# The gates' transposes ahead of the value projection, in an encoder step on one core

## The reference

```python
qm, km, vm, om, gates, cq, ckv, kr = jnp.split(h @ w_in, idx, axis=-1)
ig = gates[..., :M_HEADS]
lf = jax.nn.log_sigmoid(gates[..., M_HEADS:])
# mLSTM, per block of frames: decays from the running sum of lf, stabilised by a running max
b = jnp.cumsum(lf, axis=-1)
m = jnp.maximum(b + m0[..., None], jnp.max(D, axis=-1))
num = w_inter[..., None] * (q @ C0) + S @ v
h = num / jnp.maximum(jnp.abs(den), jnp.exp(-m))[..., None]
```

## Time and profile before

| | us |
|---|---|
| median of 3 runs | 3267.42 |
| lowest, highest | 3266.88, 3267.92 |
| the profiled execution | 3267.42 |
| its span, first to last instruction | 3265.6 |
| TensorE busy in the span | 3005.4 |
| VectorE busy | 1281.1 |
| GpSimd busy | 1000.2 |
| ScalarE busy | 561.5 |

### The profile page before, as it was taken

The page is one execution under the profiler, slowest core; times in us unless marked ns, Lnnn a source line. Parts: engine busy times, 40 slices in busy tenths (PEclk is TensorE's granted clock), DMA queues, the critical chain, the costliest instruction groups (busy, mean ns, idle before and its releaser), DMA issues.

```text
span 3265.6 us, 42745 instructions
## 1 busy us (share of the span) xinstructions
PE 3005.4 (92%) x17374; PEld 2777.7 (85%) x17374; DVE 1281.1 (39%) x1366; ACT 561.5 (17%) x844; POOL 1000.2 (31%) x474
## 2 busy tenths in 40 slices
PE   4999998988899999999879998999979999999995
PEld 3988876678799999999869987666869999999995
DVE  3433344543633323233473334355354323233326
ACT  2211233431200000000132213144221000000001
POOL 1222242224133343333312223233223433333430
PEclk9999988999999999999989999799989999999997
DMA  5112210011011111111122212000211111111111
GB/s 144 35 35 32 37 41 1 1 73 45 26 45 45 39 51 45 45 45 45 30 80 42 34 28 34 28 1 7 86 33 33 51 45 45 45 45 39 51 39 53
DMA packets 210335, 137.11 MB, mean 42 GB/s; under 512 B 49256, under 2 KB 201384, under 8 KB 209712
## 3 DMA queue, kind: packets, MB, share of 16 engines
q1 hardware_dynamic: 184672, 103.97, 12.4%
q10 hardware_dynamic: 25552, 31.64, 2.8%
HBM read 119.64 MB, written 15.94 MB: 42 GB/s over the span
## 4 chain that ended last, share of the span: by engine, by line
PE 87%; DVE 3%; DVEq 3%; ACT 3%; issue 2%; ACTq 1%; POOL 0%; POOLq 0%; DMA 0%
PE acc L493 18%; PE acc L497 17%; PE acc L496 17%; PE acc L897 5%; PE acc L901 5%; PE acc L900 5%; PE acc L842 3%; DVEq L1277 2%; PE acc L472 2%; PE acc L473 2%; PE acc L474 2%; PE acc L714 1%; PE acc L621 1%; PE acc L605 1%; PE acc L524 1%
## 5 line engine op out<-in xcount | busy, mean ns | idle before, releaser
L493 PE MATMUL acc<-act_hi,slab_hi 128*128 128x352 f32 x2928 | 964.0, 329 | 63.6 <-DVE act_lo L1262 25.8
L497 PE MATMUL acc<-act_lo,slab_hi 128*128 128x352 f32 x2928 | 950.1, 324 | 0.0
L496 PE MATMUL acc<-act_hi,slab_lo 128*128 128x352 f32 x2928 | 947.7, 324 | 0.0
L371 POOL TENSOR_TENSOR slab_hi<-slab_raw,ones 128x1024 fp32r<-128x1024 f32 x148 | 281.7, 1904 | 1285.6 <-PE acc L493 691.2
L493 PEld LDWEIGHTS acc<-act_hi,slab_hi 128*128 128x128 f32 x2928 | 556.1, 190 | 80.6 <-issue 60.2
L497 PEld LDWEIGHTS acc<-act_lo,slab_hi 128*128 128x128 f32 x2928 | 558.5, 191 | 0.0
L496 PEld LDWEIGHTS acc<-act_hi,slab_lo 128*128 128x128 f32 x2928 | 557.4, 190 | 0.0
L1619 DVE TENSOR_TENSOR branch<-acc,branch 128x1056 f32<-128x1056 f32 x176 | 221.4, 1258 | 410.3 <-PE acc L901 410.3
L373 POOL TENSOR_TENSOR slab_lo<-slab_raw,slab_hi 128x1024 fp32r<-128x1024 f32 x148 | 367.9, 2486 | 21.1
L1609 DVE TENSOR_TENSOR work<-acc,work 128x1056 f32<-128x1056 f32 x44 | 55.3, 1257 | 599.4 <-PE acc L497 599.4
L371 POOL TENSOR_TENSOR small_hi<-slab_raw,ones 128x1024 fp32r<-128x1024 f32 x46 | 88.8, 1931 | 510.4 <-PEq L904 369.5
(11 more groups left out here) (328 smaller groups left out, 4302.0 us busy)
## 6 DMA issues: line engine op xcount, KB each, us to landing
slab_raw<-in_w_ffn_in SPq DMA_DIRECT2D x88, 512.0 KB, 3.6
slab_raw<-in_w_ffn_out SPq DMA_DIRECT2D x44, 512.0 KB, 3.4
slab_raw<-in_w_in SPq DMA_DIRECT2D x40, 512.0 KB, 4.9
x_spill<-residual ACTq DMA_DIRECT2D x2, 4224.0 KB, 13.0
residual<-x_spill ACTq DMA_DIRECT2D x2, 4224.0 KB, 12.6
slab_raw<-in_w_out SPq DMA_DIRECT2D x16, 512.0 KB, 3.9
branch<-in_x_prompt ACTq DMA_DIRECT2D x4, 1024.0 KB, 9.3
out_y_prompt<-branch ACTq DMA_DIRECT2D x8, 512.0 KB, 3.0
```

What stands on the lines that cost most here:

```text
L371: pool.tensor_tensor(hi, raw, ONES[:, 0:1].broadcast_to([P, SLAB]), ALU.mult)
L493: mm = pe.matmul(out, wh, HH[:, x], start=k == 0, stop=False)
L496: pe.matmul(out, wl, HH[:, x], start=False, stop=False)
L497: mm = pe.matmul(out, wh, HL[:, x], start=False, stop=k == KT - 1)
```

## The change

In TensorE's program the value product, `first_pair(2, 0, 1, 2, (2,))`, is called after the gates' transposes and selections instead of before them. This holds for both layers, since the call stands in the layers' loop. The wait for gate_exps and the wait for set 1 go with the transposes.

```diff
                 first_pair(0, 2, 0, 1, ())
 
-                first_pair(2, 0, 1, 2, (2,))
                 pe.wait_ge(gate_exps, l * 4 + 4)
                 wait_set(l, 1, 1)
                 for c in range(CH):
                     mm = pe.transpose(PS[:, 3 * BANK + c * P:3 * BANK + (c + 1) * P], X[:, G4 + c * P:G4 + (c + 1) * P], IDN[:, :])
                 for j in range(PAIRS):
                     mm = pe.matmul(bank(6, CH, off=j * CH), SEL[:, j * P:(j + 1) * P], SMALL[0:8, 40:40 + CH], start=True, stop=True)
                 mm.then_inc(gate_turned, 1)
+                first_pair(2, 0, 1, 2, (2,))
                 first_pair(3, 1, 1, 3, (0,))
                 pe.drain().then_inc(slab_free[1], 1)
```

## The result

The changed kernel is slower: a median of 3302.8 us over four timed runs (3300.0 to 3306.0) against 3267.2 us (3266.9 to 3267.9) on the same chip, ratio 1.0108, 95% interval 1.0096 to 1.0120. That is 35.6 us more, where 29.1 were forecast; it lies above the range of 3291 to 3301. Its profiled execution took 3305.8 us, with a span of 3304.0.

The account below looks back on a forecast made before the run. TensorE, busy 92% of the span, was taken to bound the kernel. Stand, transposes, value product, lost cover and clock made 14.6 us in layer 0 and 14.5 in layer 1: 3267.4 + 14.6 + 14.5 = 3296.5, range 3291 to 3301.

Parts of the forecast that it names:

- The direction: Whole kernel: slower, given a chance of 0.96, against 0.03 for the same and 0.01 for faster.
- the clock: TensorE after the stand, each layer: half clock for 4.6 us (3.0 to 6.0), 2.1 us lost.
- the later stretches: Rest of the kernel: gains or losses from clock falls landing elsewhere, 1 us to either side.
- The stand: TensorE before the gates' transposes, layer 0: idle from 111.28 to 123.60, 12.3 us, waiting for the gates.
- The gates' time of 123.54: End of ScalarE's last gate row, L1032, in layer 0: expected to stay at 123.54 despite the change.
- The value product: TensorE, behind transposes and selections: 11.39 us from first to last matmul start at full clock.
- the lost cover: Before the output-gate product: transposes no longer hide ScalarE's emptying of set 0; 1.47 us from last to first start.
- the path: TensorE from the query product to the output-gate product: the forecast's steps without the clock term, 12.5 us a layer.
- The rival of a longer half clock: Restart after the stand: half clock not left while transposes run, 1.6 us a layer more, 3299.7 in all; chance 0.07.
- The earlier gates: Rival: VectorE and ScalarE run faster while TensorE stands, gates come up to 2 us earlier, 3292; chance 0.06.
- the overtaking: Rival: TensorE passes the waiting transposes and runs the value product, time 3267.4; not slower had chance 0.03.

Follow-up runs that it names:

- warm: Changed kernel with 70 unused matmuls of 128x352 between the query product and the gates' wait; 3289.7 us, ratio 1.0063 to the kernel before.
- turns4: Changed kernel with the gates' nine transposes done four times over, only the last nine counting; a single run, 3292.6 us.
- select_later: Changed kernel with only the four selections moved behind the value product, the transposes staying ahead; 3297.1 us, ratio 1.0083 to the kernel before.
- plain: Changed kernel with the gates' nine transposes done as ordinary float32 matmuls against the identity; 3299.3 us, ratio 1.0096 to the kernel before.

## Why the prediction was wrong

The direction, the wait and the order of size were right. One term of the sum, the clock, was mis-sized, and what the later stretches add was put too low.

- The stand: 12.3 us forecast, 12.31 and 12.29 measured. The gates' time of 123.54 held, counted from the query product: L1032 ended 12.15 us after L1026 began, before 12.21.
- The value product and the lost cover: right. The wait for L1015 is 1.14 us, as taken from the earlier trace rows, and layer 0 of `warm` shows the path without the clock at 12.5 us, as in the sum.
- **The clock: this is the step that failed.** The forecast took 4.6 us at half clock, 2.1 us lost, from four restarts that all began with dense products. Measured are 9.6 and 9.1 us. The excess over the path is 3.91 - 2.06 on the gates' block and 14.07 - 11.39 on the product, 4.5 us in layer 0 and 4.4 in layer 1, where 2.1 were forecast. The price of a microsecond at half clock held (0.46 forecast, 4.5 / 9.6 = 0.47 measured); its length did not. That is 4.7 us too little in two layers (33.8 against 29.1).
- The rival of a longer half clock had the right sign and two thirds of the size (8.0 us in place of 4.6, 1.6 us a layer, where 2.4 and 2.3 were missing), but only 0.07, and its reason was wrong as stated. I had taken from the earlier trace rows that transposes bring the clock up, and two layers of `turns4` confirmed it, after 6.1 and 5.7 us. The Trainium skill ("TensorE: Matmul & The Clock Gate", Part 4) says that work in transpose mode does not count as activity that brings the clock up; `turns4` shows the contrary. With that I stopped, and did not ask what the rest of the restart looked like. Behind nine transposes come eight passes of 9 columns. `select_later` moved only these and had the clock back after 6.1 us; `plain` changed the mode and had it down for 9.4. The half clock of 20.5 us at 450.6, over narrow passes and without a stand, was in the trace that I had.
- The later stretches: forecast at 1 us to either side. The profiled pair shows 4.6 us more in them, 3.8 of it in one late split; the timed runs of the result show 35.6 - 33.8 = 1.8 us. I had not looked at what a shift of TensorE does to the meeting of GpSimd's split with VectorE's small steps, although the row at 249.49 was in the trace of before. That this comes with the change is not shown: the kernel before has such a case too, and they move from run to run.
- The earlier gates and the overtaking: both fell. ScalarE's last row kept its length (1.16 us), and no matmul of the value product starts before the selections in either layer.

With the clock term at its measured size the sum is 3267.4 + 33.8 = 3301.2, 1.6 us below the median. The rest stays open; late splits and falls of the clock in other stretches, which land differently from run to run, are of that size.

## What to carry to other kernels

When a step moves ahead of the work that covered its wait, the first part of the price is simple: the time at which its input is there, less the time at which the engine now gets to it. The second is the restart, and it is read from what runs first behind the stand: dense products had the clock back after about 6 us here, the same stand followed by a few small and narrow passes took over 9. Work put into a stand bought back most of the second part here (7.1 us of 8.9) and none of the first, and where the wait could stay under cover, as before, neither is paid. The time to spare under that cover counts too: once TensorE gained more than 0.4 us ahead of the gates, it only waited for them.

## What was not expected of the hardware

- A VectorE step of 128x6 took 2.40 us instead of 0.17 when it began 0.01 us after a GpSimd operation of 2.39 us, and ended with it; at 252.01 in the kernel before a 128x384 step that began 0.49 us after one took 2.35 instead of 0.56, and ended 0.4 us after it. Both read two operands from SBUF. The Trainium skill ("GPSIMD Engine Reference", Specifications) says that the SBUF interfaces are shared with VectorE and that VectorE instructions with two SBUF inputs contend; the trace agrees, with 2.40 us in place of 0.17.
- Transposes alone brought the clock from 1.2 back to 2.4 GHz in 6.1 and 5.7 us. Four narrow float32 selections behind nine transposes kept it at 1.2 GHz until 5.7 us of dense product had run (127.79 to 133.5). In `warm` a stand of 1.18 us with the same block behind it was followed by a fall of 3.4 us in one layer, and one of 1.05 us by none in the other.
- The kernel before had four runs 1 us apart on one chip and 21 runs 20 us apart on another, so that for a question of 3 us the same stretch in two profiles says more than the medians.
